# Division of both heads in one tensor, first loads in smaller pieces, and conv products in pieces of 410 columns

## What is computed

```
proj = x @ w_in      # q | k | v | g_att | h_c | b_c | c_c | g_conv | gate_logits
for (window, dilation) in (128,1), (512,4), (2048,16):       # 8 heads of 64 each
    out_g, lse_g = softmax attention over keys t, t-d, ..., t-window
att   = sum_g softmax_g(lse_g) * out_g
y_att  = (att * silu(g_att)) @ w_att_out
conv   = causal_dwconv3(c_c * h_c)
y_conv = (b_c * conv * silu(g_conv)) @ w_conv_out
merged = sigmoid(gA) * y_conv + sigmoid(gB) * y_att
out    = LayerNorm(alpha * x + merged @ w_o)
```

## Time and profile before

| | us |
|---|---|
| time, median of 3 runs | 931.93 (931.74 to 932.11) |
| the profiled execution, its own time | 932.53 |
| its span on core 0, the slowest | 931.0 |
| spans of the 8 cores | 929.3 to 931.0 |
| PE busy | 895.5 (96%) |
| DVE busy | 464.9 (50%) |
| ACT busy | 371.3 (40%) |
| POOL busy | 74.1 (8%) |

### The profile page before, as it was taken

One profiled execution on the slowest core, in us unless ns is written; L12 is line 12 of the kernel. 1 busy time (PEld: TensorE's weight loads), 2 busy tenths in 40 slices (PEclk: granted clock), 3 DMA queues, 4 the chain that ended last, 5 costly groups with the idle time before them and its releaser, 6 DMA issues.

```text
span 931.0 us, 15584 instructions; the slowest of 8 cores (929.3 to 931.0 us)
## 1 busy us (share of the span) xinstructions
PE 895.5 (96%) x5814; PEld 501.5 (54%) x5904; DVE 464.9 (50%) x670; ACT 371.3 (40%) x546; POOL 74.1 (8%) x86
## 2 busy tenths in 40 slices
PE   4999999999999999999999999999999999999995
PEld 2786765558585876455544444444444444444442
DVE  3233446645465544754575455544833333333686
ACT  0103348752556235856652222222322222222575
POOL 5000000000000000000000000000000000000266
PEclk9999999999999999999999999999999999999998
DMA  9996112111200212111222122112195222200384
GB/s 127 159 162 97 24 24 35 24 24 24 47 13 1 47 24 35 24 23 24 47 43 48 26 43 46 26 38 40 24 200 156 37 38 40 40 1 1 104 282 181
DMA packets 21674, 55.83 MB, mean 60 GB/s; under 512 B 1760, under 2 KB 9952, under 8 KB 21216
## 3 DMA queue, kind: packets, MB, share of 16 engines
q0 software_dynamic: 16560, 36.97, 25.1%
q1 hardware_dynamic: 4752, 17.33, 5.4%
q10 hardware_dynamic: 288, 0.52, 0.1%
HBM read 83.39 MB, written 8.39 MB: 99 GB/s over the span
## 4 chain that ended last, share of the span: by engine, by line
PE 92%; ACT 2%; issue 2%; DMA 1%; DVE 1%; POOL 0%; DVEq 0%; ACTq 0%; POOLq 0%
PE pp L434 85%; PE pp L661 4%; PE pp L633 3%; DMA xO<-xo 1%; ACT PT L639 1%; ACT Uacc L690 1%; DVE ys L854 0%; ACT rz L692 0%; DVE PT L648 0%; DVE ob L892 0%; ACT junk L871 0%; ACT KT L499 0%; DVE Uacc L680 0%; DVE sd L861 0%; DVE ob L912 0%
## 5 line engine op out<-in xcount | busy, mean ns | idle before, releaser
L434 PE MATMUL pp<-xO,wr 128*128 128x512 bf16 x2363 | 530.3, 379 | 5.5 <-issue 2.2
L434 PEld LDWEIGHTS pp<-xO,wr 128*128 128x128 bf16 x2432 | 234.9, 98 | 280.2 <-issue 3.2
L639 ACT ACTIVATE PT<-pp 128x1024 bf16<-128x1024 f32 x96 | 93.1, 1021 | 96.1 <-PE pp L633 96.0
L434 PE MATMUL pp<-wr,xO 128*128 128x256 bf16 x768 | 89.1, 277 | 13.9 <-DMA xO<-xo 12.8
L479 DVE CAST V<-pp 128x512 bf16<-128x512 f32 (+1 forms) x74 | 48.4, 655 | 90.2 <-PE pp L434 90.1
L434 PEld LDWEIGHTS pp<-wr,xO 128*128 128x128 bf16 x768 | 81.3, 120 | 20.8 <-issue 15.0
L345 POOL DMA_DIRECT2D wr<-ws x54 | 28.8, 534 | 754.5 <-PE pp L434 596.3
L682 DVE TENSOR_TENSOR Uacc<-Uacc,pp 128x512 f32<-128x512 f32 x64 | 53.4, 871 | 66.4 <-PE pp L661 62.8
L827 DVE TENSOR_TENSOR mS<-pp,gcS 128x512 f32<-128x512 f32 x32 | 22.1, 692 | 116.8 <-PE pp L434 116.8
L648 DVE TENSOR_TENSOR PT<-PT,mk_bf 128x1024 bf16<-128x1024 bf16 x96 | 65.3, 691 | 24.5 <-ACT PT L639 22.1
L499 ACT ACTIVATE KT<-pp 128x512 bf16<-128x512 f32 x72 | 40.9, 582 | 76.9 <-PE pp L434 76.8
(11 more groups left out here) (58 smaller groups left out, 660.7 us busy)
## 6 DMA issues: line engine op xcount, KB each, us to landing
wr<-ws POOLq DMA_DIRECT2D x42, 512.0 KB, 6.0
xt<-xtok SPq DMA_DIRECT2D x16, 512.0 KB, 6.9
out<-ob SPq DMA_DIRECT2D x15, 512.0 KB, 3.0
xH<-xh POOLq DMA_DIRECT2D x4, 1024.0 KB, 57.4
wr<-ws POOLq DMA_DIRECT2D x8, 384.0 KB, 5.9
xO<-xo POOLq DMA_DIRECT2D x4, 512.0 KB, 17.1
xO<-xo POOLq DMA_DIRECT2D x2, 1024.0 KB, 33.5
wo<-wo POOLq DMA_DIRECT2D x2, 1024.0 KB, 20.7
```

Source lines behind the costliest of these rows:

```text
L434: inst = e.matmul(ps[bank][:, c0:c0 + n], lhs[k], rhs[k], start=(k == 0), stop=(k == len(lhs) - 1))
L639: S.add("act", lambda e: e.activation(out=PT[h][:, :], in_=pp[h][:, :], func=AF.Exp), writes=[("PT", h)], banks=[2 * h, 2 * h + 1])
```

## The change

Three things are changed, and the memory layout with them.

1. **Loads.** The first three weight units (`v01`, `qk01`, `v00`) are loaded in two halves each, with names ("wr", i) and ("wrb", i); pieces 0 and 1 of `xO` come in four parts, piece 2 in two. The products of round 0 are made in 4 passes for `v01`, 2 for K and Q, 2 for `v00`; round 1 in 4 passes, round 2 in 2. A read of ("wr", i) is replaced through `parts` by both halves.
2. **Division.** In steps 2, 5, 8 and 11 `uevac` is gone. DVE adds z of both heads, crosswise, to one tensor `rz` (`zadd`, right behind each `pv`) and U of both to one tensor `Uf` (`uadd`, in the next quarter, behind the masks). Ln and Exp then run once for both heads, and so does the last product. A bank of `pv` is read twice, the second time by `uadd`. The four ACT operations on 64 partitions become two on 128; the DVE operations per quarter become 6 (4 on 64 partitions, 2 on 128), from 5 (3 on 128 partitions, 2 on 64).
3. **Conv.** `xP` and `xO` lie side by side in one tensor `xC`, so that sets 2 to 7 run over 2050 tokens in 5 pieces of 410, and have no halo job. Sets 0 and 1 keep theirs.

```diff
+        for i in range(6):
+            S.parts[("wr", i)] = [("wr", i), ("wrb", i)]
+            def matmuls(self, part=0, of=1, xparts=True):
...
+                if of > 1:
+                    wres = wres if part < of // 2 else ("wrb", wres[1])
...
+        for half in range(2):
+            load_next(half)
+            load_x(True, 0, 2 * half)
+            load_x(True, 0, 2 * half + 1)
+        for i in range(2):
+            load_next(0)
+            load_next(1)
+        for q in range(4):
+            load_x(True, 1, q)
+        for q in range(2):
+            load_x(True, 2, q)
...
+            def piece(i):
+                c0, n = 410 * i, 410
...
+                return xC[:, :, 30 + c0:30 + c0 + n], c0, n, w + ([] if i else ["xP"])
...
+            def zadd(m, h, ub):
...
+                S.add("dve", lambda e: e.tensor_tensor(out=rz[us, :], in0=Uacc[zs, h, sl], in1=ps[ub][zs, :], op=ALU.add),
+                      reads=[("Uacc", h, m)], writes=[("rz", h)], banks=[ub])
+
+            def uadd(m, h, ub):
...
+            def invert():
+                S.add("act", lambda e: e.activation(out=rz[:, :], in_=rz[:, :], func=AF.Ln), reads=rzs, writes=rzs)
+                S.add("act", lambda e: e.activation(out=rz[:, :], in_=rz[:, :], func=AF.Exp, scale=-1.0), reads=rzs, writes=rzs)
...
-                for h in range(2):
-                    uevac(jj, h, pv(jj, h))
...
+                now, deferred[:] = list(deferred), []
+                for add, _, _ in now:
+                    add()
+                mid = (len(chunks[jj]) + 1) // 2
+                for i, fn in enumerate(chunks[jj]):
+                    if i == mid:
+                        for _, _, div in now:
+                            div()
                     fn()
+                    if i == 0:
+                        for _, inv, _ in now:
+                            inv()
```

More of the change, by code:

```diff
@@ L263, in build @@
         mk = at("mk_bf", take(2048), [128, MKW], BF16)
+        Uf = at("Uf", take(2048), [128, 512], F32)
         assert top[0] <= 229344, top
@@ L332, in uses_of @@
             if u[0] == "v":
-                return len(vpairs(u[2])) + (4 if u[1:] == (0, 1) else 0)
+                return len(vpairs(u[2])) + {(0, 1): 6, (0, 0): 2}.get(u[1:], 0)
             if u[0] == "qk":
@@ L553, in hc_jobs, with h_fifth, c_fifth @@
             u, ch, ci = ("hc", cc), chS[cc % NCH], cc % NCH
+            fifths = cc >= 2
+            def piece(i):
+                c0, n = 410 * i, 410
+                w = [("xO", w) for w in range(4) if c0 - 2 < 512 * w + 512 and c0 + n - 2 > 512 * w]
+                return xC[:, :, 30 + c0:30 + c0 + n], c0, n, w + ([] if i else ["xP"])
+            def h_fifth(i):
+                src, c0, n, nm = piece(i)
+                b = cmm(u, 0, src, n, nm)
+                S.add("act", lambda e: e.activation(out=hS[i % 2][:, 0:n], in_=ps[b][:, 0:n], func=AF.Copy), writes=[("hS", i % 2)], banks=[b])
+            def c_fifth(i):
+                src, c0, n, nm = piece(i)
+                b = cmm(u, 128, src, n, nm)
+                S.add("dve", lambda e: e.tensor_tensor(out=ch[:, c0:c0 + n], in0=ps[b][:, 0:n], in1=hS[i % 2][:, 0:n], op=ALU.mult),
+                      reads=[("hS", i % 2)], writes=[("chS", ci, HD[i])], banks=[b])
+            if fifths:
+                return [job(6.4, f, i) for i in range(5) for f in (h_fifth, c_fifth)]
             def halo_job():
@@ L750, in build @@
             rest = [v_job(0, 0, p1[1 + 2 * w + i]) for i in range(2)]
-            if w < 2:
+            if w < 3:
                 first = [v_job(0, 1, (blk,)) for p in pairs for blk in p]
-                first, rest = (first, kq + rest) if w == 0 else (first + kq, rest)
-                for half in range(2):
-                    for j in first:
-                        j.matmuls(half)
-                        if half:
-                            j.finish()
+                n = XPARTS[w]
+                stages = [(first + (kq if w else []), n, True)]
+                if w == 0:
+                    stages += [(kq, 2, False), ([v_job(0, 0, (blk,)) for i in range(2) for blk in p1[1 + i]], 2, False)]
+                    rest = []
+                for jobs, n, xparts in stages:
+                    for part in range(n):
+                        for j in jobs:
+                            j.matmuls(part, n, xparts)
+                            if part == n - 1:
+                                j.finish()
             else:
```

115 lines of the change are left out of this document (51 added, 64 removed).

## The result

The changed kernel takes 938.46 us (937.94 and 938.98) against 932.02 before: ratio 1.0068, 95% interval 1.0051 to 1.0085. It is slower; the forecast was no change, 931.7, and its range ended at 934.2. In the profiled execution core 2 is the last, with a span of 936.4 us of 937.94.

A forecast was written before the change was run, and what follows sets the result against it. PE, busy 895.5 of 931.0 us, was taken to bound the kernel. Loads -0.7, conv -2.0 and division +2.5 sum to -0.2: 931.7 us against the median 931.93, called no change, with a range of 929.3 to 934.2.

The forecast's parts named there:

- The division, +2.5 forecast: Division in steps 2, 5, 8, 11: -4.2 from ACT waits, then +1.7, +1.6 and +3.4 from held banks; +2.5 us.
- The gain: Steps 2 to 3 and 8 to 9: two ACT operations for four, behind the first job, remove PE's waits; -4.2 us.
- The stall of step 11, quarter 2: After a halo job of 0.41 us, the third bank is asked for at T + 2.14, comes at T + 3.74; +1.6 us.
- What comes: Division's cost: `pv` banks freed only after `uadd`, queued behind both masks on DVE; +1.7, +1.6 and +3.4 us.
- the terms of steps 2 and 8: Two-job chunks, where `pv` itself asks for held banks: 0.46, 0.39, 0.46 and 0.39 over four quarters, 1.7, twice; +3.4 us.
- PE still starts at about 12.4: Round 0: first matmul waits for both halves of `v01` and part 0 of x, so its start doesn't move.
- The rival of the working halves: Rival: PE starts near 8.7 with 512 KB landed, K and Q some 1.5 us sooner; 930.2 us; 5%.
- The smaller loads slow the stream: Rival: four extra DMAs ahead of the end of `qk01`, at 0.9 us each, +3.6; 935.3 us; 9%.
- This costs nothing: Eight added DMAs: about 5 us of issuing on an engine busy for 8% of the span, far ahead of delivery.
- The step "-0.7": Loads: core 0's 1.14 us gap ahead of round 2 goes; slowest core gains 0.7 us, range -1.1 to 0.
- The convolution, -2.0 forecast: Sets 2 to 7: 80 matmuls of 410 columns for 64 of 512 plus halo job, 0.34 less each; -2.0 us.
- The range of the terms: Loads -1.1 to 0, conv -2.0 to -1, division +1 to +3.5; together 929.8 to 933.6, not all at one end.

The follow-up runs named there:

- with the banks out of the way: Kernel before with the new division, but `uadd` right behind `zadd` for each head, loads and convolution as before: 927.77 us, 0.9957; the steps 392.67.
- the ten executions with that gap alone: New division with `uadd` right behind `zadd` except in step 11's last quarter, convolution's banks begun at 6, against the kernel before: 932.00 us, 1.0001.

## Why the prediction was wrong

The forecast was -0.2 us and +6.4 came. Three steps of it failed: the banks were followed only to the end of step 11 (+2.35), a gap of PE was priced without the clock behind it (+1.7 on the cores that it hits), and the loads were put at -0.7 where they cost 2.9. With 3.6 for the loads these come to 7.65 where 6.6 are to be explained; in the profiled execution the cores that start latest keep their clock, so none bears all three in full.

**The division, +2.5 forecast, +4.85 measured.** The gain was right: -4.2 forecast, -4.2 with the banks out of the way. The stall of step 11, quarter 2, was right too: its four quarters take 8.85, 8.62, 10.35 and 10.90 us after, 8.85, 8.46, 8.85 and 8.36 before, so +1.50 for the 1.6 forecast and +0.17 in quarter 1 for 0.28. PE at that stall:

```profile
464.08 3.18 PE L448 MATMUL pp<-xC,wr 128*128 128x512 bf16 x14 [1.34 <-DVE Uf L731]
```

Steps 2, 3, 8 and 9 are 0.25 shorter where the sum had 0.8, steps 5 and 6 are 0.93 longer where it had 1.1. What failed is the step "What comes": I looked for the held bank inside the steps, in the rotation of four, and stopped at the end of step 11. The rotation's first line in the convolution is in the diff, and the last `pv` of the program holds its bank like every other. With the rotation begun at 4, where that job doesn't meet the held bank, the steps take 399.39, the +2.5 of the forecast. With the 2.35 us of that job the banks cost 6.7 + 2.35 = 9.05 by the forecast's own terms, and 9.1 by measurement. That this fits so well is partly luck: the terms of steps 2 and 8 were too small by 0.55 (3.4, where 4.2 less 0.25 is 3.95), the others too large by 0.5 together.

**The clock.** No part of the forecast had it, neither as a term nor as a rival. A gap was priced at its own length. The fall costs another 1.7 us on the cores that it hits, four of eight in the profiled execution. As the slowest core is the time, it is paid even so: each of the ten executions with that gap alone took 931.5 us or more, and 927.77 plus 2.35 is 930.1. The Trainium skill, "TensorE: Matmul & The Clock Gate", section "A second HAM failure mode: psum-queue depth-cycling", tells of a kernel that goes round the PSUM banks and in which PE idles briefly and often between groups of matmuls, so that its clock switches to and fro. The runs agree that waits for a bank can cost the clock, and show it for a single wait, which that section doesn't describe.

**The loads, -0.7 forecast, +2.9 measured.** That the halves of the weights don't let PE begin sooner was right, but "PE still starts at about 12.4" was not: it starts at 13.96 in the mean. The rival of the working halves didn't hold: with halves awaited singly PE begins at 9.6 and the kernel is still slower than before. (Its loads are the slow ones; halves by partitions, awaited singly, weren't run.) The rival "The smaller loads slow the stream" is what happened: +1.57 at K and Q, 0.4 for each of four loads if one counts so. Its price was wrong in kind, though. I argued from 512 KB and larger loads that size matters little, but in those rows no load had its packets changed, 4096 bytes for weights and 1024 for x; the change halves those of the weights. The rival had a chance of 9% and should have had more, since the rows showed nothing of the new shape. "This costs nothing", of the eight issues on POOL, left out POOL's DRAIN, which they lengthen by 0.5 us. The step "-0.7" failed as well: the gap ahead of round 2 on one core isn't what sets the median. Of that gap the forecast says that DVE "had long been done", though DVE's copy ended at 37.55, 0.34 us before PE went on; that the load was what PE waited for fits the run with piece 2 in halves, which has no such gap.

**The convolution, -2.0 forecast, -2.08 measured** where the clock holds.

**The range of the terms.** Its lower end, 929.8, has all three terms at their low ends, its upper end, 933.6, hasn't (that would be 934.4). Either way the result lies outside it.

**The signs that were named.** K and Q after 20.5 was given as a sign of error, and came (20.76). The waits on `Uf` were to be about ten of 0.3 to 0.5 and one of 1.6; there are seven on the jobs and one on `pv`, the longest 2.2.

## What to carry to other kernels

When a change delays the reader that frees a buffer, follow that buffer to its next user everywhere, past the end of the loop and into the next stage, and recount the rotation at each seam whenever the number of jobs changes. Put the last read of a PSUM bank directly behind the matmuls that fill it, and let the work that can wait be that which holds nothing. Price a gap of TensorE with the clock that may fall behind it as well, which nearly doubled the 2.2 us here. An earlier start of an engine gained nothing here where its second load came no sooner.

## What the runs showed of the hardware

- One gap of 2.19 us in a steady stream of matmuls lowered the granted clock to 1.2 GHz on three, four and six of the eight cores in three profiled executions, and not on the others with the same gap. Gaps of 1.34, 1.38 and 1.65 us, in these kernels and the one before, did not. One of 2.26 us at the start left core 4 at full clock, where one of 2.23 took core 7 down.
- Six loads of 256 KB with rows of 2 KB brought K and Q 1.2 us later than six of 256 KB with rows of 4 KB (20.44 against 19.23, on two chips).
- Matmuls of 410 columns that begin 60 + 820 i bytes into a row run at the pace of the others: 16 in 2.78 us, 0.174 each.
- Ln and Exp of 512 columns take 0.63 us on 128 partitions and on 64.
- Each load that POOL issued more lengthened its closing DRAIN, which ends last in the span, by 0.06 to 0.1 us: 8.24 us before, 8.73 with eight more.
